# A routing stage with a lag shorter by one step, its product inside the output product, and the first tile normed in the attention's last slots

## Chip, core and metric

The kernel runs on one core of a Trainium2 chip. The metric is the device time of one execution in microseconds; the median of three runs counts. The core has TensorE (PE: matrix products and transposes, into PSUM), VectorE (DVE), ScalarE (ACT), GpSimd (POOL) and SyncE (SP, which here only issues DMAs). Each engine works through its own queue in order, and they meet at semaphores.

## What is computed

A decoder layer for 2048 tokens of width 1024: RMS norm, differential attention with 8 heads, an output product with residual add, a second RMS norm, a mixture of 32 experts (4 groups of 8: the best group, in it the best two experts), residual add, final norm. What the change touches is the end of attention and the routing:

```python
o = rms_norm(o, subln_g, 1e-5) * (1.0 - lambda_init)      # per token and head, 128 columns
x = x + o.reshape(B, S, D) @ w_out
ht = rms_norm(x, norm_ffn)
g_probs = softmax(ht @ w_group + b_group)                 # 4 groups
g_idx, g_p = argmax(g_probs), max(g_probs)
e_sel = (ht @ w_expert + b_expert).reshape(T, 4, 8)[tok, g_idx]
top_v, top_i = lax.top_k(e_sel, 2)
top_w = softmax(top_v) * g_p
# assignments are sorted by expert; each expert has its list of tokens and weights
```

## The kernel before

**Stages.** `project` makes q, k and v; `attend` does attention; `mix_and_route` does the output product, the second norm and the routing; `run_experts` the experts; `finish` the last norm. Between `attend` and the mixing stage stands a barrier of all engines: a block ends when each engine has run its program to the end, and SyncE's program in `attend` ends by waiting for the last stores of o.

**Attention.** A quad is one head and 512 queries; per head the quads come in the order 2, 0, 3, 1. Work is cut into units (128 keys of a quad), numbered n up to NU. For each unit TensorE transposes the mixed probabilities (L726), ScalarE copies them (`aT`, L587), TensorE multiplies with v (L741). After a quad ScalarE copies the result (`oT`, L594), TensorE turns it back (L749), VectorE scales it into `o_sb` (L672) and SyncE stores it to `o_rows` (L537). Each engine walks the same slots n; what stands under `if n == NU` is issued behind the slots' other work. SyncE there loads the first two tiles of o into `o_t` and the second half of the output weights into `wo_raw` (L557, L558), 3 MB, after the probabilities' ring (which has the same place in SBUF) is done with and the quad that holds the first tokens is stored (gates L551 to L561).

**Mixing and routing.** 16 tiles of 128 tokens go through a pipeline that each engine writes as `step(n, par, at)`; `has(at, lag)` says whether tile n - lag exists. The first DEEP steps and the last ones are written out, those between are a hardware loop with two steps per pass. In step n the engines do, for tiles by lag:

- lag 0: the norm of o over each head (Square L976, sum L1047, Sqrt L987, reciprocal and product L1061 and L1064), transposes into `ps_a` (L1229), the high part `oT_hi` (L994).
- lag 1: the low part `oT_lo` (L1042); the output product into `ps_b` (L1219), 48 matmuls in three terms (high by high, high by low, low by high, 16 each). It waits for `x2_set`, since `ps_b` must have been read.
- lag 2: the residual add `x2` (L1039, reads `ps_b`), Square and Sqrt (L982, L984), `h2` (L1057), its transposes into `ps_c` (L1177), the copy `h2T` (L999), which waits for the routing product of the tile before, as `h2T` has one buffer. SyncE stores x2 and h2.
- lag 3: the routing product into `ps_d` (L1190), 16 narrow matmuls, at the end of TensorE's step.
- lag 4: `choose` on VectorE (L1075 to L1094): the group, the two experts, one-hot rows `both`.
- lag 5: on TensorE `count` (L1201, L1202), which ranks each token within its expert, between the first and the second term of the output product; on ScalarE the exponential for the weights (L972); on VectorE `place` (L1102 to L1119), which makes slots and weights; on GpSimd two scatters.

VectorE's order in a step is: residual add, `oT_lo`, sum over heads, place, h2, norm of o, choose. TensorE's is: output product with count inside, transposes of o, transposes of h2, routing product (the last two swapped in the steps behind tile 15). After the last place TensorE counts once more (L1240), VectorE makes the table of blocks, and the experts begin. Before the first step 0 of ScalarE can copy `oT_hi`, it splits half of the output weights (L966).

SyncE issues the loads of the first expert's weights ahead of the loop (after step DEEP - 1), and those of the second after the last product.

Of the kernel before, what the change touches and what calls it, by code (L numbers as in the profile page):

```python
# [9 lines left out]
ALU = mybir.AluOpType  # L10
# [3 lines left out]
P = 128  # L14
# [3 lines left out]
KC = D // P  # L18
# [325 lines left out]
def attend(nc, io, keep, scratch, sem):  # L344
# [87 lines left out]
    with ExitStack() as ctx:  # L432
# [39 lines left out]
        wo_rows = io["diff_w_out"].rearrange("o (c p) n -> p (o c) n", p=P)  # L472
        CONSTANTS_AT = 40
        passed = sem("passed")
        block = ctx.enter_context(nc.Block())
# [27 lines left out]
        def _(sp):  # L503
# [8 lines left out]
            for n in range(BEGIN, END):  # L512
# [34 lines left out]
                if slot_of[last_piece[16 * (HEADS - 2) + 15]] + 1 == n:  # L547

                    gate(sp, scored, last_piece[16 * (HEADS - 2) + 15] + 1, passed)
                    sp.dma_start(keep["wo_raw"][0][:, :, :], wo_rows[:, 0:KC // 2]).then_inc(wo_in[0], 16)  # L550
                if n == NU:  # L551

                    gate(sp, mixed, mixed_parts[NR], passed)
                    g = quads.index((HEADS - 1, 0))
                    gate(sp, o_out[g % 2], 16 * (g // 2 + 1), passed)
                    for t in range(2):
                        sp.dma_start(keep["o_t"][:, t, :], scratch["o"][t * P:(t + 1) * P, :]).then_inc(o_in[t], 16)  # L557
                    sp.dma_start(keep["wo_raw"][1], wo_rows[:, KC // 2:]).then_inc(wo_in[1], 16)  # L558
# [4 lines left out]
        @block.gpsimd  # L563
        def _(pool):
            pool.memset(nil[:, :], 0.0).then_inc(nil_set, 1)
            for r in range(NR):
                pool.wait_ge(coefed, r + 1)
                for n, (c0, c1) in enumerate(parts(r)):
                    done = mixed_parts[r] + n + 1
                    pool.tensor_scalar(p1(r, c0, c1), p1(r, c0, c1), coef[:, r % 8, :], 0.0, ALU.mult, ALU.add  # L570
                                       ).then_inc(scaled, 1)
                    pool.wait_ge(scaled, done)
                    pool.tensor_tensor(p0(r, c0, c1), p0(r, c0, c1), p1(r, c0, c1), ALU.add).then_inc(mixed, 1)  # L573

        @block.scalar
        def _(act):
# [3 lines left out]
            for n in range(BEGIN, END):  # L580
# [8 lines left out]
                for g in range(NG):  # L589
                    if last_unit[g] + V_LAG == n:  # L590
                        act.wait_ge(summed, last_unit[g] + 1)
                        if g:
                            act.wait_ge(turned, turn_of["U", g - 1] + 1)
                        nc.scalar.activation(oT[:, :], ps_o[:, g % 2, :], ACT.Copy).then_inc(oT_set, 1)  # L594
                for r, m in exps[n]:
                    act.wait_ge(peaked, r + 1)
# [5 lines left out]
        def _(dve):  # L602
# [72 lines left out]
            for n in range(BEGIN, END):  # L675
# [7 lines left out]
                for r in coefs[n]:  # L683
                    weigh(r)

        @block.tensor
# [99 lines left out]
def mix_and_route(nc, io, keep, scratch, sem):  # L786

    with ExitStack() as ctx:
# [76 lines left out]
        OUT0, FREED0, ROOTED2_0, SCATTERED0 = 1, 2, 1, 16  # L865
        DEEP = 5

# [53 lines left out]
        def route_gpsimd(pool):  # L921
# [19 lines left out]
            def step(n, par, at):  # L941
                if has(at, 5):
                    t, q = n - 5, 1 - par
                    gate(pool, slot_set, t + (1 + SLOT0), passed)
# [13 lines left out]
        def route_scalar(act):  # L958
# [9 lines left out]
            def step(n, par, at):  # L968
                if has(at, 5):
                    q = 1 - par  # L970
                    act.wait_ge(chosen, (n - 5) * 13 + 13)
                    nc.scalar.activation(e5[:, q, :], x5[:, q, :], ACT.Exp).then_inc(exped, 1)  # L972
                if has(at, 0):
                    act.wait_ge(o_in[par], uses(n, par) + 16)
                    act.wait_ge(summed, n + SUMMED0)
                    nc.scalar.activation(sq[:, :], o_t[:, par, :], ACT.Square).then_inc(squared, 1)  # L976
                if has(at, 2):
# [6 lines left out]
                    nc.scalar.activation(rt2[:, :], ss2[:, :], ACT.Sqrt, bias=eps6[:, 0:1], scale=1.0 / D).then_inc(rooted2, 1)  # L984
                if has(at, 0):
                    act.wait_ge(summed, n + (1 + SUMMED0))
# [16 lines left out]
        def route_vector(dve):  # L1003
# [30 lines left out]
            def step(n, par, at):  # L1034
# [5 lines left out]
                if has(at, 1):  # L1040
# [3 lines left out]
                                                   op1=ALU.subtract).then_inc(oT_lo_set, 1)  # L1044
                if has(at, 0):
                    dve.wait_ge(squared, n + 1)
                    nc.vector.tensor_reduce(ssh[:, :], sq[:, :].rearrange("p (h e) -> p h e", h=HEADS), AX.X,  # L1047
                                            ALU.add).then_inc(summed, 1)
                if has(at, 5):
                    place(n - 5, 1 - par)  # L1050
                if has(at, 2):
# [6 lines left out]
                                                   in1=g2_row[:, :], op0=ALU.mult, op1=ALU.mult).then_inc(h2_set, 1)  # L1058
                if has(at, 0):
                    dve.wait_ge(rooted, n + 1)  # L1060
# [5 lines left out]
                if at == 0:  # L1066
                    split_low(range(KC // 2))
                if has(at, 4):
                    choose(n - 4, par)

# [94 lines left out]
        def route_tensor(pe):  # L1165
# [28 lines left out]
            def count(n, par, at):  # L1194
                if has(at, 5):
                    t, q = n - 5, 1 - par
                    if at == 5:
                        pe.wait_ge(made, 11)
# [5 lines left out]
            def step(n, par, at):  # L1204
                if has(at, 1):
# [4 lines left out]
                    for o, w in ((oT_hi, wo_hi), (oT_hi, wo_lo), (oT_lo, wo_hi)):  # L1210
                        if k == KC:
                            count(n, par, at)
                        if o is oT_lo:
# [8 lines left out]
                    mm.then_inc(projected, 1)  # L1222
                else:
                    count(n, par, at)
                if has(at, 0):
# [4 lines left out]
                    mm.then_inc(turned, 1)  # L1230
                if at < TILES:
                    turn_h2(n, par, at)
                    route(n, at)
                else:
                    route(n, at)
                    turn_h2(n, par, at)

# [477 lines left out]
```

## Time and profile before

| | before |
|---|---|
| median of 3 runs | 2501.5 us |
| lowest, highest | 2501.24, 2504.43 us |
| the profiled execution, its own time | 2500.24 us |
| span of its profile | 2498.7 us |
| TensorE busy over the span | 92% |
| VectorE busy | 55% |
| ScalarE busy | 48% |
| GpSimd busy | 30% |

Times in the profile are microseconds from the span's start; L with a number is a line of the kernel. A line of the timeline gives start, duration, engine, line, operation, what is written from what, shape, count, and in brackets the idle time ahead of it and what ended it. PEld is TensorE's loading of weights. The granted clock of TensorE is given as a share of 2.4 GHz. A duration is that of the instruction; consecutive ones on an engine overlap by some hundredths. The tensor names are shortened: `p_ring` also stands for `o_t` and half of `wo_raw`, which lie in its place, `x` for `x2`, `h` for `h2`.

### The profile page before, as it was taken

Reading aid. Unit: us, or ns where it says so; the run is one execution under the profiler, and the core shown is the slowest. Engines: PE = TensorE matmul, PEld = TensorE weight load, DVE = VectorE, ACT = ScalarE, POOL = GpSimd, SP = SyncE. Lnnn points to the kernel's source line nnn. Section 1 sums busy time; section 2 is a strip of 40 time slices with the busy share of each in tenths; the row PEclk is TensorE's granted clock in tenths of the full one; section 3 lists DMA queues with packets and bytes.
Section 4 is the critical chain, followed back from the end, with each engine's and each line's share of the span. In section 5 each row is a group of like instructions: output and inputs, shape, how many; then the busy total and the mean of one; then the engine's idle time right before and its main releaser. Section 6 shows DMA issues by size and latency. Waiting matters only on the chain. (4 is left out here: it accounts for less than half of the span.)

```text
span 2498.7 us, 36865 instructions
## 1 busy us (share of the span) xinstructions
PE 2297.3 (92%) x11480; PEld 1843.1 (74%) x11480; DVE 1382.9 (55%) x2803; ACT 1209.7 (48%) x1636; POOL 761.7 (30%) x686
## 2 busy tenths in 40 slices
PE   4999999998999999999979997599999999999980
PEld 3888888997667676766658886477888888788760
DVE  6212121002877777777635776577655565666763
ACT  5111111112777777777743443475545464655653
POOL 0000000001887777777700111222222222222220
PEclk8999999999999999999989998799999999999995
DMA  5333334223643544354135455589887878888957
GB/s 194 135 109 118 126 118 145 68 64 86 157 101 90 133 106 102 84 121 118 30 117 201 128 138 179 203 296 356 288 286 234 286 228 285 304 291 287 319 151 286
DMA packets 207630, 441.46 MB, mean 177 GB/s; under 512 B 19082, under 2 KB 56114, under 8 KB 205491
## 3 DMA queue, kind: packets, MB, share of 16 engines
q1 hardware_dynamic: 188530, 379.46, 45.9%
q0 software_dynamic: 19008, 60.91, 9.7%
q8 instruction: 42, 0.69, 0.1%
q14 instruction: 50, 0.40, 0.1%
HBM read 338.55 MB, written 101.76 MB: 176 GB/s over the span
## 5 line engine op out<-in xcount | busy, mean ns | idle before, releaser
L1446 DVE TENSOR_TENSOR gu_lo<-gu_raw,gu_hi 128x2048 fp32r<-128x2048 f32 x128 | 293.3, 2291 | 119.9 <-issue 83.0
L573 POOL TENSOR_TENSOR p_ring<-p_ring 128x512 f32<-128x512 f32 (+2 forms) x192 | 334.6, 1743 | 16.0
L633 DVE TENSOR_SCALAR_CACHE_REDUCE p_ring<-ps_s 128x512 f32<-128x512 f32 (+6 forms) x352 | 276.9, 791 | 98.0 <-PE ps_s L704 88.5
L598 ACT ACTIVATE p_ring<-p_ring,shift 128x1152 f32<-128x1152 f32 (+15 forms) x256 | 305.8, 1197 | 21.9 <-DVE shift L649 21.9
L741 PE MATMUL ps_o<-aT,v_st 128*128 128x512 f32 (+3 forms) x640 | 285.5, 530 | 0.0
L587 ACT ACTIVATE aT<-ps_t 128x512 f32<-128x512 f32 (+1 forms) x320 | 168.9, 530 | 168.7 <-PE ps_t L726 167.5
L1523 PE MATMUL ps_g<-gu_hi,xT_lo 128*128 128x512 f32 x720 | 235.9, 409 | 8.2 <-DVE xT_lo L1461 8.2
L1386 ACT ACTIVATE gu_hi<-gu_raw 128x2048 fp32r (+1 forms) x128 | 237.9, 1916 | 9.2 <-PE ps_g L1523 4.8
L1523 PE MATMUL ps_g<-gu_lo,xT_hi 128*128 128x512 f32 x720 | 227.4, 397 | 0.0
L1523 PE MATMUL ps_g<-gu_hi,xT_hi 128*128 128x512 f32 x720 | 227.3, 397 | 0.0
L570 POOL TENSOR_SCALAR p_ring<-p_ring,coef 128x512 f32<-128x512 f32 (+2 forms) x192 | 168.1, 875 | 129.8 <-DVE coef L662 127.8
L258 DVE TENSOR_TENSOR stage<-ps,stage 128x512 fp32r<-128x512 f32 x64 | 44.3, 692 | 274.6 <-ACT stage L205 274.6
L1454 DVE TENSOR_TENSOR d_lo<-d_raw,d_hi 128x2048 fp32r<-128x2048 f32 x64 | 146.7, 2292 | 84.5 <-ACT d_hi L1393 50.4
L1350 POOL DMA_INDIRECT x_rows<-y_sb,lists x45 | 100.2, 2227 | 300.6 <-ACT y_sb L1404 279.6
L205 ACT ACTIVATE stage<-ps 128x512 fp32r<-128x512 f32 x64 | 38.3, 598 | 312.9 <-PE ps L321 312.9
L726 PE MATMUL ps_t<-ident,p_ring 128*128 128x128 f32 x1088 | 171.6, 273 | 0.6 <-ACT aT L587 0.4
L1414 ACT ACTIVATE act_g<-ps_g 128x512 f32<-128x512 f32 x45 | 27.0, 600 | 292.6 <-PE ps_g L1523 292.6
L726 PEld LDWEIGHTS ps_t<-ident,p_ring 128*128 128x128 f32 x1088 | 132.9, 140 | 37.9 <-issue 15.0
L1523 PEld LDWEIGHTS ps_g<-gu_lo,xT_hi 128*128 128x128 f32 x720 | 136.5, 190 | 32.9
L1523 PEld LDWEIGHTS ps_g<-gu_hi,xT_hi 128*128 128x128 f32 x720 | 135.9, 189 | 32.9
L1523 PEld LDWEIGHTS ps_g<-gu_hi,xT_lo 128*128 128x128 f32 x720 | 129.8, 190 | 35.3 <-issue 7.7
L704 PE MATMUL ps_s<-k,q_first 128*128 128x512 f32 (+1 forms) x448 | 141.4, 441 | 14.7 <-DVE top L636 7.0
(217 smaller groups left out, 4363.8 us busy)
## 6 DMA issues: line engine op xcount, KB each, us to landing
gu_raw<-in_moe_w_gate SPq DMA_DIRECT2D x128, 512.0 KB
gu_raw<-in_moe_w_up SPq DMA_DIRECT2D x128, 512.0 KB
d_raw<-in_moe_w_down SPq DMA_DIRECT2D x64, 1024.0 KB
qk<-stage SPq DMA_DIRECT2D x64, 512.0 KB, 2.8
q_first<-qk SPq DMA_DIRECT2D x64, 256.0 KB, 5.0
q_second<-qk SPq DMA_DIRECT2D x64, 256.0 KB, 5.1
w_raw<-in_diff_w_in POOLq DMA_DIRECT2D x12, 1024.0 KB, 6.8
k<-qk SPq DMA_DIRECT2D x8, 1024.0 KB, 12.2
```

The lines of the kernel that those rows point to most:

```text
L570: pool.tensor_scalar(p1(r, c0, c1), p1(r, c0, c1), coef[:, r % 8, :], 0.0, ALU.mult, ALU.add).then_inc(scaled, 1)
L573: pool.tensor_tensor(p0(r, c0, c1), p0(r, c0, c1), p1(r, c0, c1), ALU.add).then_inc(mixed, 1)
L587: nc.scalar.activation(aT[:, n % A_RING, a0 * P:], ps_t[:, turn_of["T", n] % 2, a0 * P:], ACT.Copy).then_inc(t_out, 1)
L598: nc.scalar.activation(p, p, ACT.Exp, bias=shift[:, r % 8, m:m + 1], accum_out=sums[:, r % 8, m:m + 1]).then_inc(raised, 1)
L633: ins = nc.vector.tensor_scalar(p(r, k0, k0 + far), ps_s[:, c % 2, 0:far], SCALE, None, ALU.mult, ALU.max, accum_out=top[:, r % 4, m, col: ...
L704: mm = pe.matmul(ps_s[:, c % 2, j:j + e], q_st[g % 2][:, hl, m, a * P:(a + 1) * P], k_st[h % 2][:, m, k0 + j:k0 + j + e], start=hl == 1, s ...
L726: mm = pe.transpose(ps_t[:, t % 2, a * P:(a + 1) * P], p0(4 * g + a, k * P, (k + 1) * P), ident[:, :])
L741: pe.matmul(ps_o[:, g % 2, a0 * P:], v_st[:, h % 2, k, :], aT[:, u % A_RING, a0 * P:], start=k == 0, stop=last).then_inc(summed, 1)
L1386: nc.scalar.activation(gu_hi[:, j * GC:(j + 1) * GC], raw(half, j), ACT.Copy).then_inc(gu_hi_set, 1)
L1446: nc.vector.tensor_tensor(gu_lo[:, j * GC:(j + 1) * GC], raw(half, j), gu_hi[:, j * GC:(j + 1) * GC].bitcast(F32), ALU.subtract).then_inc( ...
L1454: nc.vector.tensor_tensor(d_lo[:, j * DC:(j + 1) * DC, :], d_raw[:, j], d_hi[:, j * DC:(j + 1) * DC, :].bitcast(F32), ALU.subtract).then_i ...
L1523: mm = pe.matmul(ps_g[:, half, :], x[:, cs], w[:, c, half, :], start=c == 0 and k == 0, stop=c == KC - 1 and k == 2)
```

## The change

The shorter lag: choose goes from lag 4 to 3, and exponential, count, place and scatters from 5 to 4, so that DEEP is 4 and there is one step less behind the last tile. The routing product (lag 3 as before) goes from the end of TensorE's step into the output product, ahead of the count. In the steps without an output product it stands with the count at the front. The buffer index of the moved parts changes with the lag's parity.

The first tile: SyncE's loads of two o tiles and half of the output weights are issued eight slots earlier. ScalarE does the Square of the first o tile in slot NU - 3 and the Sqrt in slot NU - 1 of attention, VectorE the sum over heads in slot NU - 2 and the norm in slot NU; GpSimd sets the constant 1e-5 at its row 8. Places that are free by then serve (`v_st`, `lq`). The semaphores carry on into the mixing stage, whose step 0 has these four instructions no more.

```diff
--- before.py
+++ after.py
@@ -471,6 +471,12 @@
         gain_in, const_in, o_in = sem("c_gain_in"), sem("c_const_in"), [sem("c_o_in0"), sem("c_o_in1")]
         wo_rows = io["diff_w_out"].rearrange("o (c p) n -> p (o c) n", p=P)
         CONSTANTS_AT = 40
+
+        o_first, o_sq = keep["o_t"][:, 0, :], v_st[:, HEADS % 2, 0:KC, :].rearrange("p c e -> p (c e)")
+        o_sums, o_root, o_inv, eps_o = lq[:, 0, 0:HEADS], lq[:, 1, 0:HEADS], lq[:, 2, 0:HEADS], lq[:, 3, 0:1]
+        o_squared, o_summed, o_rooted, o_inverted, o_normed = (
+            sem("c_" + n) for n in ("squared", "summed", "rooted", "inverted", "normed"))
+        eps_set = s("eps")
         passed = sem("passed")
         block = ctx.enter_context(nc.Block())
 
@@ -548,7 +554,7 @@
 
                     gate(sp, scored, last_piece[16 * (HEADS - 2) + 15] + 1, passed)
                     sp.dma_start(keep["wo_raw"][0][:, :, :], wo_rows[:, 0:KC // 2]).then_inc(wo_in[0], 16)
-                if n == NU:
+                if n == NU - 8:
 
                     gate(sp, mixed, mixed_parts[NR], passed)
                     g = quads.index((HEADS - 1, 0))
@@ -564,6 +570,8 @@
         def _(pool):
             pool.memset(nil[:, :], 0.0).then_inc(nil_set, 1)
             for r in range(NR):
+                if r == 8:
+                    pool.memset(eps_o, 1e-5).then_inc(eps_set, 1)
                 pool.wait_ge(coefed, r + 1)
                 for n, (c0, c1) in enumerate(parts(r)):
                     done = mixed_parts[r] + n + 1
@@ -592,6 +600,14 @@
                         if g:
                             act.wait_ge(turned, turn_of["U", g - 1] + 1)
                         nc.scalar.activation(oT[:, :], ps_o[:, g % 2, :], ACT.Copy).then_inc(oT_set, 1)
+                if n == NU - 3:
+                    act.wait_ge(o_in[0], 16)
+                    act.wait_ge(summed, last_unit[4 * (HEADS - 2) + 3] + 1)
+                    nc.scalar.activation(o_sq, o_first, ACT.Square).then_inc(o_squared, 1)
+                if n == NU - 1:
+                    act.wait_ge(eps_set, 1)
+                    act.wait_ge(o_summed, 1)
+                    nc.scalar.activation(o_root, o_sums, ACT.Sqrt, bias=eps_o, scale=1.0 / P).then_inc(o_rooted, 1)
                 for r, m in exps[n]:
                     act.wait_ge(peaked, r + 1)
                     p = (p0, p1)[m](r, 0, (rows[r][1] + 1) * P)
@@ -682,6 +698,16 @@
                         out(g)
                 for r in coefs[n]:
                     weigh(r)
+                if n == NU - 2:
+                    dve.wait_ge(o_squared, 1)
+                    nc.vector.tensor_reduce(o_sums, o_sq.rearrange("p (h e) -> p h e", h=HEADS), AX.X, ALU.add).then_inc(o_summed, 1)
+                if n == NU:
+                    dve.wait_ge(o_rooted, 1)
+                    nc.vector.reciprocal(o_inv, o_root).then_inc(o_inverted, 1)
+                    dve.wait_ge(o_inverted, 1)
+                    by_head = o_first.rearrange("p (h e) -> p h e", h=HEADS)
+                    nc.vector.tensor_tensor(by_head, by_head, o_inv.unsqueeze(2).to_broadcast([P, HEADS, P]),
+                                            ALU.mult).then_inc(o_normed, 1)
 
         @block.tensor
         def _(pe):
@@ -863,7 +889,7 @@
 
         TURNED0, OT_LO0, PROJECTED0, X2_0, H2T0, ROUTED0, BOTH0, SLOT0, SUMMED0 = 2, 1, 2, 1, 1, 1, 1, 1, 1
         OUT0, FREED0, ROOTED2_0, SCATTERED0 = 1, 2, 1, 16
-        DEEP = 5
+        DEEP = 4
 
         def steps(eng, step, after_first=None, before_loop=None):
 
@@ -939,8 +965,8 @@
             pool.wait_ge(scattered[1], SCATTERED0)
 
             def step(n, par, at):
-                if has(at, 5):
-                    t, q = n - 5, 1 - par
+                if has(at, 4):
+                    t, q = n - 4, par
                     gate(pool, slot_set, t + (1 + SLOT0), passed)
                     for k in range(2):
                         pool.indirect_dma_start(scratch["slots"], bass.IndirectOffsetOnAxis(ap=slot[:, q, k:k + 1], axis=0),
@@ -966,11 +992,11 @@
                     nc.scalar.activation(wo_hi[:, c, :], wo_raw[2 * c // KC][:, c % (KC // 2), :], ACT.Copy).then_inc(wo_hi_set, 1)
 
             def step(n, par, at):
-                if has(at, 5):
-                    q = 1 - par
-                    act.wait_ge(chosen, (n - 5) * 13 + 13)
+                if has(at, 4):
+                    q = par
+                    act.wait_ge(chosen, (n - 4) * 13 + 13)
                     nc.scalar.activation(e5[:, q, :], x5[:, q, :], ACT.Exp).then_inc(exped, 1)
-                if has(at, 0):
+                if has(at, 0) and at > 0:
                     act.wait_ge(o_in[par], uses(n, par) + 16)
                     act.wait_ge(summed, n + SUMMED0)
                     nc.scalar.activation(sq[:, :], o_t[:, par, :], ACT.Square).then_inc(squared, 1)
@@ -982,7 +1008,7 @@
                     nc.scalar.activation(sq2[:, :], x2[:, par, :], ACT.Square, accum_out=ss2[:, :]).then_inc(squared2, 1)
                     act.wait_ge(squared2, t + 1)
                     nc.scalar.activation(rt2[:, :], ss2[:, :], ACT.Sqrt, bias=eps6[:, 0:1], scale=1.0 / D).then_inc(rooted2, 1)
-                if has(at, 0):
+                if has(at, 0) and at > 0:
                     act.wait_ge(summed, n + (1 + SUMMED0))
                     nc.scalar.activation(rth[:, :], ssh[:, :], ACT.Sqrt, bias=eps5[:, 0:1], scale=1.0 / P).then_inc(rooted, 1)
                 if at == 0:
@@ -1042,12 +1068,12 @@
                     nc.vector.scalar_tensor_tensor(out=oT_lo[:, 1 - par, :], in0=ps_a[:, :], scalar=sub_gs[:, 0:1],
                                                    in1=oT_hi[:, 1 - par, :].bitcast(F32), op0=ALU.mult,
                                                    op1=ALU.subtract).then_inc(oT_lo_set, 1)
-                if has(at, 0):
+                if has(at, 0) and at > 0:
                     dve.wait_ge(squared, n + 1)
                     nc.vector.tensor_reduce(ssh[:, :], sq[:, :].rearrange("p (h e) -> p h e", h=HEADS), AX.X,
                                             ALU.add).then_inc(summed, 1)
-                if has(at, 5):
-                    place(n - 5, 1 - par)
+                if has(at, 4):
+                    place(n - 4, par)
                 if has(at, 2):
                     t = n - 2
                     dve.wait_ge(rooted2, t + (1 + ROOTED2_0))
@@ -1056,7 +1082,7 @@
                     dve.wait_ge(h2_out[par], uses(t, par) + OUT0)
                     nc.vector.scalar_tensor_tensor(out=h2[:, par, :], in0=x2[:, par, :], scalar=ri2[:, 0:1],
                                                    in1=g2_row[:, :], op0=ALU.mult, op1=ALU.mult).then_inc(h2_set, 1)
-                if has(at, 0):
+                if has(at, 0) and at > 0:
                     dve.wait_ge(rooted, n + 1)
                     nc.vector.reciprocal(rih[:, :], rth[:, :]).then_inc(inverted, 1)
                     dve.wait_ge(inverted, n + 1)
@@ -1065,8 +1091,8 @@
                                             ALU.mult).then_inc(normed, 1)
                 if at == 0:
                     split_low(range(KC // 2))
-                if has(at, 4):
-                    choose(n - 4, par)
+                if has(at, 3):
+                    choose(n - 3, 1 - par)
 
             def choose(t, q):
 
@@ -1192,9 +1218,9 @@
                     mm.then_inc(routed, 1)
 
             def count(n, par, at):
-                if has(at, 5):
-                    t, q = n - 5, 1 - par
-                    if at == 5:
+                if has(at, 4):
+                    t, q = n - 4, par
+                    if at == 4:
                         pe.wait_ge(made, 11)
                     pe.wait_ge(both_set, t + (1 + BOTH0))
                     pe.wait_ge(slot_set, t + SLOT0)
@@ -1209,6 +1235,7 @@
                     k = 0
                     for o, w in ((oT_hi, wo_hi), (oT_hi, wo_lo), (oT_lo, wo_hi)):
                         if k == KC:
+                            route(n, at)
                             count(n, par, at)
                         if o is oT_lo:
                             pe.wait_ge(oT_lo_set, t + (1 + OT_LO0))
@@ -1221,6 +1248,7 @@
                             k += 1
                     mm.then_inc(projected, 1)
                 else:
+                    route(n, at)
                     count(n, par, at)
                 if has(at, 0):
                     pe.wait_ge(normed, n + 1)
@@ -1228,12 +1256,7 @@
                     for c in range(KC):
                         mm = pe.transpose(ps_a[:, c * P:(c + 1) * P], o_t[:, par, c * P:(c + 1) * P], ident[:, :])
                     mm.then_inc(turned, 1)
-                if at < TILES:
-                    turn_h2(n, par, at)
-                    route(n, at)
-                else:
-                    route(n, at)
-                    turn_h2(n, par, at)
+                turn_h2(n, par, at)
 
             steps(pe, step)
             pe.wait_ge(slot_set, TILES + SLOT0)
```

## Rows read from the trace of the kernel before

**Rows 1.** Windows: busy us (instructions) by engine, granted clock, DMA share, GB/s.

```profile
1333.12:1518.94 185.82, 182.17 (x1007) 156.82 (x1006) 131.30 (x468) 85.92 (x117) 28.20 (x22) 0.99 0.51 152
1518.94:1565.77 46.83, 26.39 (x134) 23.84 (x133) 26.74 (x151) 17.19 (x22) 8.54 (x8) 0.69 0.53 187
```

**Rows 2.** Timeline of the seam between attention and mixing, by engine.

```profile
1269.83 0.49 ACT L587 ACTIVATE aT<-ps_t 128x384 f32<-128x384 f32 x1 [0.59 <-PE ps_t L726]
...
1271.88 0.28 ACT L587 ACTIVATE aT<-ps_t 128x128 f32<-128x128 f32 x1 [0.59 <-PE ps_t L726]
...
1274.53 0.69 DVE L672 TENSOR_TENSOR o_sb<-ps_t,inv 128x512 f32<-128x512 f32 x1 [5.62 <-PE ps_t L749]
...
1275.31 0.40 SPq L537 DMA_DIRECT2D o_rows<-o_sb  x1
...
1282.41 1.06 ACT L976 ACTIVATE sq<-p_ring 128x1024 f32<-128x1024 f32 x1 [8.63 <-POOL ones L925]
...
1283.48 1.28 ACT L987 ACT_TABLE_LOAD   x1
...
1284.98 3.88 ACT L966 ACTIVATE wo_hi<-wo_first 128x1024 fp32r<-128x1024 f32 x4
```

**Rows 3.** Waits of SyncE's queue at the seam: total us, times, longest.

```profile
SPq L561 <- DMA o_rows<-o_sb: 5.0, 1, 5.0
```

**Rows 4.** The stores of o (L537, 32 of them), from issue to landing.

```profile
DMA to landing us min/median/max: 2.3/2.6/15.1
```

**Rows 5.** Timeline of the mixing loop: steps around 1331, 1379, 1411 to 1442.

```profile
1331.41 1.87 PE L1190 MATMUL ps_d<-w_r,h2T 128*128 128x36 f32 x16
...
1333.12 3.92 PE L1219 MATMUL ps_b<-wo_hi,oT_hi 128*128 128x512 f32 x16
...
1379.02 5.28 PE L1219 MATMUL ps_b<-wo_hi,oT_hi 128*128 128x512 f32 x15 [0.68 <-DVE x L1039]
...
1411.56 3.89 PE L1219 MATMUL ps_b<-wo_hi,oT_hi 128*128 128x512 f32 x16 [0.59 <-DVE x L1039]
...
1416.03 0.19 DVE L1102 CUSTOM_DVE_ANT_0 junk<-own,ps_e 128x32 f32<-128x32 f32 x1 [0.21 <-PE ps_e L1202]
...
1425.40 1.22 DVE L1039 TENSOR_TENSOR x<-ps_b,x 128x1024 f32<-128x1024 f32 x1
...
1426.77 3.92 PE L1219 MATMUL ps_b<-wo_hi,oT_hi 128*128 128x512 f32 x16
...
1431.42 0.18 DVE L1102 CUSTOM_DVE_ANT_0 junk<-own,ps_e 128x32 f32<-128x32 f32 x1
...
1441.10 1.22 DVE L1039 TENSOR_TENSOR x<-ps_b,x 128x1024 f32<-128x1024 f32 x1 [0.41 <-issue]
...
1442.00 1.03 ACT L999 ACTIVATE h2T<-ps_c 128x1024 f32<-128x1024 f32 x1 [1.53 <-PE ps_d L1190]
```

**Rows 6.** Timeline from the last output product to the last place.

```profile
1518.94 3.90 PE L1219 MATMUL ps_b<-wo_hi,oT_hi 128*128 128x512 f32 x16
...
1523.43 0.19 DVE L1102 CUSTOM_DVE_ANT_0 junk<-own,ps_e 128x32 f32<-128x32 f32 x1 [3.44 <-PE ps_e L1202]
...
1527.15 0.16 DVE L1075 TENSOR_TENSOR lg<-ps_d,b_r 128x4 f32<-128x4 f32 x1
...
1530.42 1.87 PE L1190 MATMUL ps_d<-w_r,h2T 128*128 128x36 f32 x16
...
1540.25 3.60 PE L1190 MATMUL ps_d<-w_r,h2T 128*128 128x36 f32 x16 [6.69 <-DVE le L1076]
...
1543.65 1.95 PE L1177 MATMUL ps_c<-ident,h 128*128 128x128 f32 x8
...
1546.51 0.19 DVE L1102 CUSTOM_DVE_ANT_0 junk<-own,ps_e 128x32 f32<-128x32 f32 x1 [2.59 <-PE ps_e L1202]
...
1555.13 0.19 DVE L1102 CUSTOM_DVE_ANT_0 junk<-own,ps_e 128x32 f32<-128x32 f32 x1 [1.33 <-PE ps_e L1202]
...
1565.60 0.17 DVE L1119 CAST slot<-slot_f 128x2 int32<-128x2 f32 x1
```

## The prediction

> **What bounds the kernel now.** I read the windows by stage first, then the timeline of the mixing stage, engine by engine, and last the waits of SyncE at the seam between attention and mixing. Call T(n) the moment at which TensorE starts the output product of step n (the product of token tile n-1). The windows [rows 1] show the mixing stage from T(4) to T(16) with TensorE busy 182.17 of 185.82 us, so twelve steps of 15.5 us on average look TensorE-bound. The timeline says that this is a tie. In the step that starts at 1411.56, VectorE's placing chain starts at 1416.03, and what released it was TensorE's count product; VectorE then runs without a rest until its residual add `x` at 1425.40, and the next product starts at 1426.77, which is 1.37 us after the start of that add, about its length [rows 5]. So there is a ring through two engines: T(n), first third of the product, count, place, h2, norm of the next o tile, choose, residual add, T(n+1). The add is queued behind choose on VectorE, and TensorE waits for it because the add frees `ps_b`. The ring takes 4.47 + 9.37 + 1.37 = 15.21 us; TensorE's own work fills nearly the same time. Where the loop branches back, the add has 0.41 us of issue idle ahead of it [rows 5].
>
> **The routing product moved inside the output product.** Now the routing product stands behind the transposes at the end of a step. It costs TensorE 1.71 us (its start at 1331.41 to the next product at 1333.12) [rows 5]. Afterwards it stands between the first and the second third, ahead of the count. TensorE issues the same instructions per step; only their order changes. But everything behind it in that queue shifts by 1.71 us, and the count is what VectorE's place waits for. T(n) to place becomes 4.47 + 1.71 = 6.18 us, and the rest of the ring (9.37 + 1.37) consists of the same instructions in the same order, with choose now working on a tile one step younger. The new ring: 16.92 us, and 17.33 where the loop branches.
>
> The move does take something off: ScalarE's copy `h2T` waited 1.53 us for the routing product of the tile before [rows 5], and no longer will, so Square and the sum over heads come that much sooner. They end ahead of place, which in the new order waits for the count anyway, so I cost that gain at nothing; without that cover it would be worth at most those 1.53 us. What takes over the time that TensorE saves at the end of a step is an idle wait for the residual add, some 2 us in each step. Waits of the moved product itself are met early: its `h2T` was copied at the end of the step before, and its `ps_d` was read at the head of choose.
>
> Twelve steps from T(4) to T(16) have all parts. Ten are in the loop (five passes, four branches between them within this stretch): 12 x 16.92 + 4 x 0.41 = 204.7 us, against 185.82 now [rows 1]. That is +18.9. In the trace of before, one of these steps has a slow first third: 5.28 us for 15 matmuls at 1379.02, against 3.90 for 16 [rows 5, 6], so about 1.6 us of lowered clock is in the 185.82. If it comes again, the loss is 20.5; if the two steps written out behind the loop run a little shorter than those in it, as little as 18.3. I take **+19.2 us**. The steps ahead of T(4) have no place yet, and the routing product's 1.71 us is in TensorE's queue either way: nothing.
>
> **One step less at the end.** From T(16) to the last tile's slots the trace has 46.83 us [rows 1]: four further steps without output product, in which choose and place alternate. With the shorter lag there are three. Written out after T(16) with rows of before [rows 6]: place(12) starts at 4.49 + 1.71 = 6.2; choose(13) 3.72 later at 9.9. The product ends at 1530.42 - 1518.94 = 11.5, plus 1.71 = 13.2. Then the transposes of h2(14) take about 1 us (half of the cold 1.95) to 14.2, the copy 1.03 [rows 5] to 15.3, the routing product 1.71 to 17.0, the count, and place(13) starts at about 18.1; choose(14) at 21.8, and h2(15) is ready at the same time. TensorE by then has idled some 4 us, so I take cold durations from the same stretch of before: from the start of the transposes of h2 to place 2.86 us (1543.65 to 1546.51), plus the copy and the routing product (3.40, from 1540.25 to 1543.65), which now stand between them: with 0.2 for the added hand-over, place(14) starts at 29.3. From there the old trace has exactly what is left, place(14), choose(15), place(15): 1555.13 to 1565.60 and 0.17 more, 10.64 us. Sum 39.9, against 46.83: -6.9, and I take **-6.8 us**. With a warm clock the transposes and the routing product would be 2.6 us shorter (-9.4); with a delay of 1 us for scatters that land late beside the weight loads, -5.8. All behind it (counts, table, first gather, experts) keeps its length.
>
> **The first o tile ahead of the seam.** Three things change here.
> (a) SyncE issues the 3 MB of loads (two o tiles, half of the output weights) at the first unit of the last quad, not after its last. Now they are in the queue ahead of the last store of o (issued at 1275.31), and SyncE waits 5.0 us for that store [rows 2, 3]. The 32 stores of this kind have a median of 2.6 us from issue to landing, least 2.3 [rows 4]. With the loads landed long before, the last store should behave like the median: 5.4 - 2.6 = 2.8 us off. Bounds: 0 and 3.1.
> (b) Square, Sqrt and the norm now run inside attention. ScalarE can do Square behind the copy at 1269.83, which leaves the next two copies in time. Sqrt comes behind the last aT copy (ends 1272.16) and needs a table load: 1.50 us from the load to the next instruction, as at 1283.48 to 1284.98 [rows 2], so it is done at about 1273.7. VectorE's reciprocal follows and a multiplication over 128x1024, about as long as the residual add (1.22) [rows 5], to 1275.2, and the last o output, which started at 1274.53, is queued behind them on VectorE: +0.7 us on the last store. GpSimd's memset of one column is hidden under its waits in the first rows of attention.
> (c) The mixing stage's ScalarE starts at once with splitting the output weights, not with Square (1282.41) and the table load: the split begins 2.57 us sooner (1284.98 - 1282.41) [rows 2], and the first transposed tile is copied behind it, then the product starts. TensorE's transposes of the normed tile, and SyncE's loads, are done by then.
> Sum of the seam: -2.8 + 0.7 - 2.57 = **-4.7 us**; bounds -1.9 and -5.0.
> On (b) the Trainium skill would charge more: its page "ScalarE: Activation LUTs", section "What ACT_TABLE_LOAD costs", adds a drain of about 1.38 us to each load of 1.28 us. By that, the seam would come to -3.3 as an estimate from the page. The trace shows the 1.28 us load and no such gap beside it, so I keep to the row.
>
> **Sum.** +19.2 - 6.8 - 4.7 = +7.7 us. The profiled execution took 2500.24 us (span 2498.7), the median of the runs is 2501.5. So 2507.9 for one like the profiled, and **2509.2 us** for the median.
>
> **Rivals.**
> *The ring gives way and TensorE's work is all that is left (faster).* In other steps of before place began without any wait, as at 1431.42 [rows 5], so there ScalarE's side was as late as TensorE's. If place were released by ScalarE's earlier Square and not by the count, the loop would fall to TensorE's own 182 us of work. It decides at the point where routing product and count end sooner than 4.6 us after T(n); the rows give 6.2, so it would need the routing product to cost almost nothing inside the product. It would give 2501.5 - 3.6 - 6.8 - 4.7 = 2486 us; a half of it 2498. Chance 0.09.
> *The ring loses, but less.* The moved 1.71 us is partly absorbed (1.2 instead of 1.6 us a step), or the tail has a warm clock: 19.2 becomes 14, or the tail -9.4. Then net +2 to +5, 2504 to 2506. Chance 0.2.
> *The clock.* Two spots of weak activity in each step now (narrow routing matmuls with the count inside the product, and the idle wait of 2 us ahead of it) stand for one before. The trace has one drop to half clock in twelve such steps, worth 1.6 us [rows 5]. If a drop hit each first third, it would be 12 x 1.6 = +19 us more: 2528; in four steps of twelve, 2516. Against it: each of those twelve steps already had 1.7 us of narrow matmuls and some idle time in one piece, longer together than either spot now, and eleven kept the full clock. The Trainium skill, "TensorE: Matmul & The Clock Gate", section "A second HAM failure mode: psum-queue depth-cycling", says that frequent short pauses between groups of matmuls can make the clock go back and forth; that is this rival, and the one drop in the trace agrees with it weakly. Chance 0.13.
> *My forecast*, 0.58, with a range of its own of 2506 to 2514.
>
> **Chances and range.** A change under 0.2% (5 us) can hardly be told from none here. Slower than 2506.5: nearly all of the forecast (0.54) and the clock's case: 0.67. Within 0.2%: the milder loss and the edges: 0.24. Faster: 0.09. The range that leaves out 2 in 10 reaches over the milder loss and part of the clock's case, with the seam's bounds at its ends: 2501 to 2518.
>
> **What the changed profile would show.** The step period in the loop near 17 us; every first place instruction released by TensorE's count, none free; place 6.2 us after T(n); TensorE idle about 2 us ahead of each product and released by `x`; the granted clock of the loop still near 0.99. At the seam: the last store landing under 3 us, first split of ScalarE at about 1280.3, first product 4.7 us sooner than before. From T(16) to the last slots 40 us. The prediction fails if the period is 15.2 or less, if place starts within 5 us of T(n), or if the seam or the tail gains twice what I give it.

## The result and the profile after

The changed kernel takes 2512.2 us (median of 5 runs, 2511.7 to 2516.3) against 2501.6 us (2501.2 to 2504.4): ratio 1.0047, 95% interval 1.0035 to 1.0059. It is slower by 10.6 us; 2509.2 was forecast, with 2501 to 2518 as the range.

The windows by stage of the changed kernel, with the columns of [rows 1]. The first is from T(1) to T(4), then T(4) to T(16), then to the last place:

```profile
1287.57:1330.58 43.01, 41.14 (x201) 34.15 (x201) 27.09 (x49) 14.39 (x21) 0.60 (x1) 0.97 0.43 158
1330.58:1537.35 206.77, 183.94 (x1009) 156.80 (x1009) 134.91 (x481) 88.52 (x122) 30.66 (x24) 0.99 0.45 132
1537.35:1577.73 40.38, 24.24 (x128) 21.20 (x128) 21.55 (x118) 15.63 (x20) 6.72 (x6) 0.74 0.52 187
```

The stretch from T(4) to T(16), called the loop below (its last two steps are written out behind the hardware loop), took 206.77 us where it took 185.82 [rows 1], while TensorE's busy time in it hardly grew (183.94 us against 182.17). The tail, from T(16) to the last place, is 6.5 us shorter. The timeline of one step shows why; it answers to [rows 5]:

```profile
1418.20 3.89 PE L1246 MATMUL ps_b<-wo_hi,oT_hi 128*128 128x512 f32 x16 [1.81 <-DVE x L1065]
1421.93 1.87 PE L1216 MATMUL ps_d<-w_r,h2T 128*128 128x36 f32 x16
1423.63 0.39 PE L1227 MATMUL ps_e<-before,ones 128*128 128x32 f32 x2
...
1424.46 0.19 DVE L1128 CUSTOM_DVE_ANT_0 junk<-own,ps_e 128x32 f32<-128x32 f32 x1 [3.16 <-PE ps_e L1228]
...
1434.13 1.23 DVE L1065 TENSOR_TENSOR x<-ps_b,x 128x1024 f32<-128x1024 f32 x1 [0.41 <-issue]
...
1435.50 3.92 PE L1246 MATMUL ps_b<-wo_hi,oT_hi 128*128 128x512 f32 x16 [2.12 <-DVE x L1065]
```

Place starts 6.26 us after the product, was idle for 3.16 us until TensorE's count came, and the next product then waits 2.12 us for the residual add. The period is 17.30 us with the loop's branch in it. The waits of VectorE and TensorE from T(4) to T(16) (total us, times, longest):

```profile
DVE junk L1128 <- PE ps_e L1228: 39.6, 12, 5.0
DVE ssh L1073 <- ACT sq L1002: 10.0, 12, 2.1
...
PE ps_b L1246 <- DVE x L1065: 22.8, 12, 2.3
```

All twelve places are released by the count. In the same stretch of before it was five of eleven places and 2.7 us, TensorE's waits for the residual add came to 3.2 us in six steps, and the sum over heads waited 28.1 us for ScalarE's Square.

At the seam, the timeline and SyncE's waits:

```profile
1273.56 1.22 DVE L703 TENSOR_REDUCE lq<-v_st 128x8 f32<-128x1024 f32 x1 [2.40 <-ACT v_st L606]
...
1274.86 1.28 ACT L610 ACT_TABLE_LOAD   x1 [0.44 <-DVE lq L703]
1276.16 0.30 ACT L610 ACTIVATE lq<-lq 128x8 f32<-128x8 f32 x1
1276.36 0.58 ACT L602 ACTIVATE oT<-ps_o 128x512 f32<-128x512 f32 x1
...
1276.99 0.66 PE L775 MATMUL ps_t<-ident,oT 128*128 128x128 f32 x4 [1.59 <-ACT oT L602]
1277.87 0.69 DVE L688 TENSOR_TENSOR o_sb<-ps_t,inv 128x512 f32<-128x512 f32 x1
1281.46 0.10 POOL L948 MEMSET eps<- 128x1 f32 x1 [31.73 <-POOLq L432]
...
1282.62 3.90 ACT L992 ACTIVATE wo_hi<-wo_first 128x1024 fp32r<-128x1024 f32 x4 [5.68 <-POOL ones L951]
...
SPq L567 <- DMA o_rows<-o_sb: 1.9, 1, 1.9
```

Attention's first store of o is issued at 676.5 us here and at 674.1 in the profile of before. Ahead of it the edit adds one instruction, GpSimd's memset of 0.10 us at 644.0; the last experiment shows that the kernel before varies as much between two of its own profiles. At the end of attention the shift is 2.26 us (its last output but one starts at 1270.47 and, before, at 1268.21), and I take that off. Net of it, the last o output is 1.1 us later (1274.53 to 1277.87), the last store's wait is 1.9 in place of 5.0 us [rows 3], and ScalarE's first split of the output weights comes 4.6 us sooner (1284.98 to 1282.62) [rows 2].

### The profile page after: what moved, and what is told of

It reads as the page before. It is cut to its first block and busy times, and to the rows that moved or that the text cites. A ratio compares the mean times of both kernels' runs of the same rounds, so it can differ in the third digit from the quotient of the medians.

```text
span 2510.7 us, 36864 instructions
## 1 busy us (share of the span) xinstructions
PE 2298.5 (92%) x11480; PEld 1840.5 (73%) x11480; DVE 1384.0 (55%) x2803; ACT 1210.6 (48%) x1638; POOL 763.6 (30%) x687
```

## Experiments

Each run was timed beside the kernel before on its own chip; medians of before there are 2500.9 to 2501.8. T(n) and periods are read from the timeline of each.

**Which part costs.** Two kernels with one part each: the routing part (DEEP = 4, lags, routing product in front of the count), with attention and step 0 as before, and the seam part (early loads, first tile normed in attention) with lags and TensorE's order as before.

> The routing part of the change alone; the end of attention and step 0 as in the kernel before. Ring theory (the routing product delays the count, the count releases place, and place leads through choose and the residual add to the next product): the step period stays at 17.0 us, 17.3 where the loop branches, T(4) to T(16) some 21 us longer than before, the tail from T(16) to the last place 6.5 us shorter, sum +14.4 us: 2516 us. Rival (the seam's extra work in attention is what costs, by more than the trace seems to say): this kernel is near 2501 us or below.

> The seam part alone; lags and order of the mixing stage as before. By the two traces the first output product comes 4.6 us sooner (last store of o lands 2.8 us sooner, is issued 1.0 later, ScalarE's first split comes 2.6 us sooner in the mixing stage, 0.2 lost elsewhere) and nothing behind it changes: 2497 us. Rival (the gain is given back in the loop or at its end): 2501.6 us with the loop or the tail some 4.6 us longer.

The routing part took 2518.6 us (ratio 1.0068, 1.0054 to 1.0082), the seam part 2498.0 (0.9981, 0.9972 to 0.9990). T(4) to T(16) was 206.6 us with the routing part and 184.2 with the seam part, the tail 40.9 and 46.8 us. The losses and gains stand where the theory puts them and don't disturb each other: the two ratios make 1.0049 together, and the whole change has 1.0047. The seam part's loop is 1.6 us shorter than before because no first third of its twelve ran at the lowered clock. The routing part measured 16.7 us slower by medians where 14.4 was expected, and the interval holds both; its stretch from T(4) to the end of the tail is longer by 14.8 us.

**Is it the count's place, or the narrow matmuls inside the product?** Count and routing product swapped:

```diff
                         if k == KC:
-                            route(n, at)
                             count(n, par, at)
+                            route(n, at)
```

> The changed kernel with count and routing product swapped inside the output product: count first, then the routing product. The same instructions, the same lags. Ring theory: place starts 4.5 to 4.9 us after T(n) again, the period falls from 17.0 to between 15.2 and 15.7 us, the loop costs what it did before (186 us from T(4) to T(16)), and seam and tail keep their gains of 4.6 and 6.5 us: 2491 us, 21 below the changed kernel. Rival (narrow matmuls in the middle of the output product cost TensorE time or clock, wherever they stand in it): the period stays at 17 us and the time at 2512.

And the count a third later still:

```diff
                         if k == KC:
                             route(n, at)
+                        if k == 2 * KC:
                             count(n, par, at)
```

> The changed kernel with the count behind the second third of the output product, the routing product still behind the first. Ring theory: the count ends a third of a product later (3.63 us), so place starts 9.8 us after T(n) and the period is 20.5 us, 20.9 at branches: twelve steps cost 43.6 us more, 2556 us. Rival (the count's place doesn't matter, the routing product does): 2512 us.

With the count first it is 2491.5 us (0.9960, 0.9946 to 0.9973): 10.4 us faster than the kernel before, 20.8 faster than the changed one, with the same instructions. One step of it:

```profile
1394.45 3.88 PE L1246 MATMUL ps_b<-wo_hi,oT_hi 128*128 128x512 f32 x16 [0.37 <-ACT oT_hi L1020]
...
1398.92 0.19 DVE L1128 CUSTOM_DVE_ANT_0 junk<-own,ps_e 128x32 f32<-128x32 f32 x1
...
1409.94 3.95 PE L1246 MATMUL ps_b<-wo_hi,oT_hi 128*128 128x512 f32 x16 [0.33 <-ACT oT_hi L1020]
```

Place starts 4.47 us after T(n), and no idle time stands ahead of it. The loop took 186.75 us and the tail 40.4. The rival on narrow matmuls fell, since they stand inside the product here too. Of the 20.95 us that the loop had lost, 20.0 are gone with the order of these two lines; about 1.7 of those are the one drop of the clock, which the changed kernel had in the loop and this one had not. What is left against the seam part alone, also without a drop, is 2.5 us (186.75 against 184.2); the next question is about it.

The other way it is 2578 us (median of two runs), well over the 2556 expected. In the steps with a full clock the mechanism is right: step 4 took 20.91 us, step 15 20.43, with place 9.97 us after T(n). In the ten between, the period was 21.9 to 23.8 us, and the first thirds look like this:

```profile
1352.85 6.52 PE L1247 MATMUL ps_b<-wo_hi,oT_hi 128*128 128x512 f32 x16 [2.28 <-DVE x L1065]
1376.61 6.59 PE L1247 MATMUL ps_b<-wo_hi,oT_hi 128*128 128x512 f32 x16 [3.89 <-DVE x L1065]
1399.95 5.25 PE L1247 MATMUL ps_b<-wo_hi,oT_hi 128*128 128x512 f32 x16 [3.35 <-DVE x L1065]
```

Windows of that kernel around the third of them; the last three columns are granted clock, DMA share, GB/s:

```profile
1398.00:1399.00 1.00, 0.00 (x0) 0.00 (x0) 0.93 (x4) 1.00 (x1) 0.00 (x0) 1.00 1.17 283
1399.00:1400.00 1.00, 0.05 (x1) 0.09 (x1) 1.00 (x2) 0.99 (x3) 0.00 (x0) 0.72 1.07 201
1400.00:1401.00 1.00, 1.00 (x3) 0.81 (x4) 1.00 (x2) 1.00 (x2) 0.00 (x0) 0.50 0.89 221
```

TensorE had been idle for 3.35 us, and the clock fell to 1.2 GHz just before the product began. The first third and the count behind it in the queue then take longer, and since both are in the ring, place comes 11.3 to 12.8 us after T(n). So my rival of the clock is a real mechanism. In the changed kernel it happened once in twelve steps, as it did before the change:

```profile
1347.82 5.50 PE L1246 MATMUL ps_b<-wo_hi,oT_hi 128*128 128x512 f32 x16 [2.04 <-DVE x L1065]
...
1366.87 3.88 PE L1246 MATMUL ps_b<-wo_hi,oT_hi 128*128 128x512 f32 x16 [2.26 <-DVE x L1065]
```

The length of the wait ahead of a product does not decide it alone: the product after 2.04 us was slow (period 19.05), the next one, after 2.26, was not, and in the kernel with the late count one after 2.28 us was slow, while those at T(15) and T(16) kept the full clock after 3.28 and 3.27. What else decides is not shown.

**What holds the period at 15.55 us with the count first?** That kernel's products are no longer released by the residual add but by `oT_hi`. TensorE's waits from 1350 to 1510 in it:

```profile
PE ps_b L1246 <- ACT oT_hi L1020: 3.0, 9, 0.4
PE ps_b L1246 <- DVE x L1065: 0.5, 1, 0.5
```

Four kernels on this: the count ahead of the first third; the transposes of the next o tile moved into the last third (from the kernel with the count first), one without and one with Square ahead of the exponential on ScalarE; and all three together. In the cut below, `turn_o` holds the lines of these transposes that stood behind the product.

```diff
                         for c in range(KC):
+                            if o is oT_lo and c == KC // 2 and has(at, 0):
+                                turn_o(n, par)
...
-                if has(at, 0):
+                if has(at, 0) and not has(at, 1):
...
```

> The changed kernel with the count ahead of the first third of the output product (it needs only choose of the step before), the routing product behind the first third. Ring theory: the count no longer releases place; place starts behind ScalarE's Square and the sum over heads, near 4.7 us after T(n), so the ring is no shorter than with the count in the middle. With the copy oT_hi as TensorE's releaser, as in the run with the count first, the period is 15.5 us: 2491 us, no different from that run. Rival (each delay of the count is paid in full, so a count 3.8 us sooner pays too): period near 13 us or TensorE's bare 15.0, 2484 us.

> The run with the count first, and in it the transposes of the next o tile moved into the middle of the last third of the output product, so that ScalarE's copy oT_hi is done when the next product is due. With the count first each product waited 0.33 us for oT_hi, and its period was 15.55 us; the routing product at the end of the step used to cover that copy. Theory (a lost cover of 0.65 us in each step from the third on): step 3 takes 14.5 us in place of 15.1, the steps behind it 15.2 to 15.4, now bound by the ring through place again: 2487 to 2490 us. Rival (the 0.65 us are the price of narrow matmuls inside the product): step 3 stays at 15.1 and the time at 2491.

> The run before (count first, transposes of o early), and ScalarE does Square of o ahead of the exponential with its table load, in each step. If ScalarE's side of the ring is what holds the period at 15.2 to 15.4, the sum over heads ends 1.5 us sooner, the count alone leads, and the period is 15.2 (15.6 at branches): 2487 us. If not, no difference from the run before.

> All three: the count ahead of the first third, transposes of o early, Square ahead of the exponential. Both leads of place are shortened (place at about 3.4 us after T(n)), so the ring takes 14.1 us and TensorE's own work of 14.9 to 15.0 us a step is the bound: T(4) to T(16) 180 us, 2484 us. Rival (the residual add or VectorE's own queue still leads): the period stays at 15.2.

| kernel | median us, ratio (95%) | step 3, us | period, us | product waits for (us) |
|---|---|---|---|---|
| count ahead of the product | 2492.0, 0.9958 (0.9943 to 0.9974) | 15.75 | 15.56, 15.73 | `oT_hi`, under the count |
| transposes of o early | 2495.4, 0.9975 (0.9964 to 0.9985) | 15.32 | 15.76 | residual add, 0.54 |
| the same, Square first | 2494.8, 0.9977 (0.9966 to 0.9987) | 15.28 | 15.76 | residual add, 0.54 |
| all three | 2487.2, 0.9946 (0.9932 to 0.9960) | 15.21 | 15.23 | nothing, 0.15 in the last steps |

The first came out in time and period as the ring theory said (2491 and 15.5 were expected): a count that comes sooner than the sum over heads buys nothing. Place came 3.9 to 4.0 us after T(n), not 4.7, with no idle time ahead of it. The second did not: I expected step 3 at 14.5 us and 2487 to 2490, and T(4) to T(16) took 189.3 us, 2.6 more than with the count first. Its timeline shows a shorter dependency that I had left out:

```profile
1360.89 2.08 PE L1255 MATMUL ps_b<-wo_hi,oT_lo 128*128 128x512 f32 x8
...
1362.80 1.04 PE L1203 MATMUL ps_c<-ident,h 128*128 128x128 f32 x8
1363.01 1.23 DVE L1065 TENSOR_TENSOR x<-ps_b,x 128x1024 f32<-128x1024 f32 x1 [0.53 <-PE ps_b L1255]
...
1364.38 3.92 PE L1255 MATMUL ps_b<-wo_hi,oT_hi 128*128 128x512 f32 x16 [0.54 <-DVE x L1065]
```

The residual add reads `ps_b`, starts when the product ends, and has to end before the next starts: 1.58 us from 1362.80, where the product makes way for the transposes of h2, to 1364.38. What TensorE does in between must cover that. The transposes of o did, and without them only those of h2 are left (1.04 us). VectorE waits for the end of the product at that point (0.53 us), not for its own chain. So Square first changed nothing in the time, and its interval overlaps the run without, though the sum over heads did end some 1.5 us sooner: place's wait for the count grew from 0.25 to 1.78 us. With the count at that spot as well (all three together) the 1.58 us are covered nearly, TensorE has no wait in most steps, and the period of 15.23 is its own work, where I had put 14.9 to 15.0. So T(4) to T(16) took 183.0 us and not 180, and the time is 2487.2 and not 2484. That kernel has the lowest median of all, 0.54% (0.40 to 0.68) under the kernel before. Against the one with the count first the intervals overlap; in the traces its loop is 3.8 us shorter. None of the four got step 3 to 14.5 us. The changed kernel's own timeline splits its 0.65 us (15.12 against 14.47): from T(3) to the transposes of o 12.87 us against 11.02, which is 1.85 for a routing product that cost 1.71 at the end of a step, and from those transposes to T(4) 2.25 us against 1.74 without the routing product. So 0.14 us is the price of standing inside, and 0.51 that of the lost cover.

**The seam's parts.** Only `if n == NU:` of SyncE's loads made `if n == NU - 8:` in the kernel before, and the kernel before once more.

> The kernel before, with SyncE's 3 MB of loads for the mixing stage issued eight slots earlier and nothing else. Theory (the last store of o queued behind these loads): it lands 2.3 us after its issue in place of 5.4, the mixing stage starts 3.1 us sooner against that store's issue, and nothing else moves: 2498.7 us. Rival (the barrier between the stages, or the load of code for the next, sets the start): the store lands sooner and the mixing stage's first instructions do not; 2501.6 us.

> The kernel before once more, for its profile. In the traces of the changed kernels attention's first store is issued 2.4 to 3.6 us later than in the profile of before, though nothing ahead of it was edited. If that is variation between executions, this profile shows it later than 674.1 us too, or at least the spread of the projection's start; the mixing stage then has the same steps: 186 us from T(4) to T(16), less 1.6 us if no drop of the clock falls into it. If the edits behind it moved it, the first store is at 674.1 again.

```profile
1280.80 0.10 POOL L922 MEMSET eps<- 128x1 f32 x1 [30.67 <-POOLq L432]
...
1281.24 0.10 POOL L922 MEMSET eps<- 128x1 f32 x1 [33.81 <-POOLq L432]
```

The first of these lines is of the kernel with early loads, the second of before. With the early loads alone the store's wait is 1.9 us, and the mixing stage's first instruction comes at 1280.80, 3.6 us after the last o output started (1277.20); before, it was 1281.24 - 1274.53 = 6.7 us. So 3.1 us, and the rival of the barrier fell. The run took 2499.85 us, ratio 0.9988 (0.9979 to 0.9998); the interval holds both the 3.1 us and nearly nothing, so here the profile speaks and not the time. The kernel before, profiled again, has its first store at 677.0 us and T(1) at 1293.21, 3.3 us later than in its first profile, while T(4) to T(16) is 185.86: the shift ahead of attention is variation between executions. The kernel with the routing part alone, whose attention is that of before, has its first store at 676.8 too. In the second profile of before the wait for the last store is 5.4 us and not 5.0, so what the early loads save is known to some 0.4 us.

## Why the prediction was right, and where it was off

| term | predicted | measured |
|---|---|---|
| seam, to T(1) | -4.7 | -4.6 (after the shift of 2.3) |
| T(1) to T(4) | 0 | -0.2 |
| T(4) to T(16) | +19.2 | +20.95 |
| T(16) to the last place | -6.8 | -6.5 |
| sum | +7.7 | +9.65 |

**The ring** was right, and is shown: take the 1.71 us out of its path and the loss of the loop goes (count first), put another third of the product into it and the full-clock steps grow by as much (T(4) by 3.67 us, T(15) by 3.67, for a third of 3.63). Predicted were 16.92 us a step and 17.33 with a branch; measured 16.97 to 17.01, and 17.30 to 17.35, with 17.24 in the first step, 16.76 in the last two, and 19.05 in the one with the drop of the clock. What remains of the term: the drop of the clock came again, the case for which the prediction gives +20.5, while its sum took +19.2. Of the other 0.45 us, part is place, which came 6.28 and not 6.18 us after T(n).

**The idle wait of 2 us** ahead of each product is there (22.8 us in twelve).

**T(1) to T(4)**, costed at nothing, hides two errors that nearly cancel. Step 3 took 15.12 us, was 14.47: at the end of a step the routing product had covered ScalarE's copy of `oT_hi`, which my working for the steps ahead of T(4) left out. Later the ring's wait hides it. Step 1 took 14.62 us, was 15.45, since the clock rose sooner in its first third (5.28 against 6.12 us for the 16 matmuls). TensorE's earlier transposes in step 0 do not explain it: the kernel with early loads only, whose step 0 is the old one, had 5.44 us, and with the new step 0 the kernel with early transposes had 6.15 and the one with the late count 6.80. What sets this stays open, so this gain is luck. The two errors nearly cancel by chance.

**The seam** came to -4.6 us where -4.7 was forecast, with two errors that cancel. Net of the shift, the mixing stage's first instruction came 3.1 us sooner after the last o output, where I took the median of the stores (2.8); that output was 1.1 us later and not 0.7; and the split came 2.6 us sooner against that first instruction, as forecast. The lines of before beside those above:

```profile
1273.83 0.66 PE L749 MATMUL ps_t<-ident,oT 128*128 128x128 f32 x4 [0.69 <-ACT oT L594]
...
1283.50 1.22 DVE L1047 TENSOR_REDUCE ssh<-sq 128x8 f32<-128x1024 f32 x1 [1.12 <-ACT sq L976]
```

The delay of the last output has the step that was off: the prediction lets the table load begin as the last `aT` copy ends. It began 0.44 us later, only when the sum over heads had come, while at 1283.48 before, it ran under the wait for that sum [rows 2]. Why it did so once and not the other time stays open. The prediction also follows one path only, VectorE's queue. ScalarE's copy `oT` of the last quad stands behind the Sqrt too, so TensorE's last transposes start 0.9 us later net of the shift (1273.83 to 1276.99); an empty VectorE would have saved 0.2 us at most, as an estimate from these rows. The load took 1.28 us with 0.02 behind it, so the drain of 1.38 us that the Trainium skill ("ScalarE: Activation LUTs", "What ACT_TABLE_LOAD costs") adds does not show here either.

**The tail** follows the hand-made timeline within 0.4 us (place(14) starts 29.7 us after T(16) where 29.3 was written), with the clock down from the transposes of h2(15) on, as assumed:

```profile
1559.27 1.97 PE L1203 MATMUL ps_c<-ident,h 128*128 128x128 f32 x8 [4.07 <-DVE h L1083]
1562.35 3.63 PE L1216 MATMUL ps_d<-w_r,h2T 128*128 128x36 f32 x16 [1.11 <-ACT h2T L1025]
```

The two profiled executions are 12.0 us apart, and the 9.65 of these terms with the shift of 2.3 make that up: nothing behind the last place changed. Between the medians it is 10.6 us; the forecast is 3.0 us short of the changed kernel's median, of which 1.95 are in the terms, nearly all of it in the loop's.

## What to carry to other kernels

When two engines look busy in turn, write down the ring of waits through both and its length before moving anything: an instruction put ahead of one that another engine waits for can cost its full duration in every step, as here (1.7 us in each of twelve), though neither engine got more work. Where a product is moved into another, put what someone waits for first. And ask of each move what the moved work was covering where it stood; here it was a copy, and in a later experiment a residual add.

## What was not expected of the hardware

In the changed kernel TensorE's clock stood idle waits of 1.6 to 2.3 us per step with one drop to 1.2 GHz in twelve steps. With the count still later it fell in ten of twelve, nine times after idle waits of 3.3 to 3.9 us and once after 2.28, each costing 1.4 to 2.9 us since the slow matmuls are in the ring. The two waits of 3.3 us ahead of T(15) and T(16) did not lower it. With all full-clock and slow steps together, a delay of 3.6 us a step cost 5.3.
